# One layer of a hybrid encoder with 32 experts: the front part, up to the first projection, is redone

## What is computed

```python
cond = silu(c)
mod = cond @ w_ada + b_ada                     # D_MODEL = 1024, six parts
h = rmsnorm(x, norm1_g) * (1.0 + sc1) + sh1    # x: 256 x 1024
proj = h @ w_in + b_in
# the filters of the Hyena branch, which depend on no input x
hdn = sin(freq * (z @ w1 + b1))                # 256 x 64
hdn = sin(freq * (hdn @ w2 + b2))
hdn = sin(freq * (hdn @ w3 + b3))
filt = (hdn @ w4) * window                     # 256 x 2 orders x 2 directions x 512
# used as spectra: y = irfft(rfft(u) * rfft(kern))
```

## Time and profile before

| | us |
|---|---|
| median of three runs | 1292.68 |
| lowest and highest | 1291.25 to 1293.13 |
| the profiled execution: its time | 1291.79 |
| the profiled execution: its span | 1290.0 |

### The profile page before, as it was taken

How to read it: one execution, slowest core, us unless ns; L and a number is a source line. 1 busy time by engine, 2 the same in 40 slices (tenths; PEclk the granted TensorE clock), 3 DMA queues, 4 the chain that set the end, 5 groups by cost and what they waited for, 6 DMA issues and landing times.

```text
span 1290.0 us, 13991 instructions
## 1 busy us (share of the span) xinstructions
PE 1213.5 (94%) x5550; PEld 577.2 (45%) x5550; DVE 410.2 (32%) x774; ACT 174.0 (13%) x311; POOL 33.1 (3%) x50
## 2 busy tenths in 40 slices
PE   6999999999999999999999998999899999989897
PEld 1777478888544343333333332433333333334332
DVE  5178896884422221120222102111301211021203
ACT  3222004230221010010101001000101010010000
POOL 3300200001000000000000000000000000000000
PEclk9999999999999999999999999999999999999999
DMA  9943442779489999999999999999999999999996
GB/s 373 383 174 108 148 156 107 301 286 401 179 354 426 401 428 428 428 429 428 428 430 429 427 428 429 428 428 430 429 428 428 429 428 428 430 429 427 427 426 247
DMA packets 50707, 475.73 MB, mean 369 GB/s; under 512 B 3970, under 2 KB 4130, under 8 KB 24051
## 3 DMA queue, kind: packets, MB, share of 16 engines
q1 hardware_dynamic: 49426, 471.26, 87.8%
q0 software_dynamic: 1248, 4.03, 0.9%
HBM read 474.22 MB, written 1.05 MB: 368 GB/s over the span
## 4 chain that ended last, share of the span: by engine, by line
PE 66%; DMA 28%; DVE 2%; ACT 1%; issue 1%; SPq 0%; DVEq 0%
DMA ring_sb<-w_down 26%; PE bank L1149 20%; PE bank L1249 11%; PE bank L859 10%; PE bank L1104 5%; PE bank L1265 4%; PE bank L1020 3%; PE bank L868 3%; PE bank L1049 2%; DMA area_sb<-w_down 2%; PE bank L1118 1%; DVE area_sb L1867 1%; PE bank L784 1%; PE bank L798 1%; PE bank L1010 1%
## 5 line engine op out<-in xcount | busy, mean ns | idle before, releaser
L1149 PE MATMUL bank<-ring_sb,area_sb 128*64 128x512 f32 x1536 | 400.2, 598 | 16.4 <-DMA ring_sb<-w_gu 16.4
L1149 PEld LDWEIGHTS bank<-ring_sb,area_sb 128*64 128x64 f32 x1536 | 124.4, 137 | 226.1 <-issue 213.7
L1249 PE MATMUL bank<-ring_sb,area_sb 128*64 128x512 f32 x608 | 165.9, 598 | 18.7 <-DMA ring_sb<-w_down 16.8
L1149 PE MATMUL bank<-area_sb 128*64 128x512 f32 x512 | 171.2, 594 | 0.0
L859 PE MATMUL bank<-area_3h_sb,ring_sb 128*128 128x256 f32 x704 | 154.2, 379 | 0.0
L859 PEld LDWEIGHTS bank<-area_3h_sb,ring_sb 128*128 128x128 f32 x704 | 133.2, 190 | 20.1 <-issue 1.8
L2123 DVE TENSOR_SCALAR area_sb<-bank 128x512 f32<-128x512 f32 x32 | 22.1, 692 | 304.2 <-PE bank L1149 304.2
L2147 DVE TENSOR_TENSOR area_sb<-area_sb,bank 128x512 f32<-128x512 f32 x64 | 44.0, 688 | 211.9 <-PE bank L1265 211.9
L2154 DVE TENSOR_TENSOR area_sb<-bank,area_sb 128x512 f32<-128x512 f32 x32 | 22.1, 692 | 230.4 <-PE bank L1249 218.0
L1249 PEld LDWEIGHTS bank<-ring_sb,area_sb 128*64 128x64 f32 x608 | 51.2, 137 | 89.7 <-issue 89.7
L1509 ACT ACTIVATE area_sb<-bank 128x512 f32<-128x512 f32 (+1 forms) x80 | 44.0, 551 | 333.5 <-PE bank L1104 255.6
(11 more groups left out here) (278 smaller groups left out, 807.8 us busy)
## 6 DMA issues: line engine op xcount, KB each, us to landing
ring_sb<-w_gu SPq DMA_DIRECT2D x96, 2048.0 KB, 26.2
ring_sb<-w_down SPq DMA_DIRECT2D x38, 2048.0 KB, 25.8
area_sb<-w_gu SPq DMA_DIRECT2D x32, 2048.0 KB, 30.3
area_sb<-w_down SPq DMA_DIRECT2D x16, 2048.0 KB, 20.4
ring_sb<-w_in SPq DMA_DIRECT2D x14, 2048.0 KB, 10.1
ring_sb<-w_ada SPq DMA_DIRECT2D x12, 2048.0 KB, 10.3
area_3h_sb<-w_down SPq DMA_DIRECT2D x8, 2048.0 KB, 35.6
ring_sb<-w_branch SPq DMA_DIRECT2D x3, 2048.0 KB, 9.5
```

The lines of the kernel that those rows point to most:

```text
L1149: ins = pe.matmul(bank[n][r, :], xT[:, k, r], w[e][:, n * 512:(n + 1) * 512], start=False, stop=k == KT - 1, skip_group_check=True)
L1249: ins = pe.matmul(bank[4 + n][r, :], hidT[:, k, e * SLOTS:(e + 1) * SLOTS], w[e][:, kk, n * 512:(n + 1) * 512], start=False, stop=k == KT ...
```

## The change

- **Angles in turns.** The frequency is scaled by 1/(2 pi) once, so a layer's angle comes in turns; its nearest whole number is subtracted and ScalarE's sine takes the factor -2 x 3.1415925. Three VectorE steps a layer in place of seven.
- **Constant products.** TensorE multiplies `ones` by `ones` (128 columns) six, seven and nine times ahead of and between the network's products, into the bank of `ada3`, which a later product with its start flag clears.
- **Order.** TensorE: `mlp(2)`, `ada(0)`, filters, `ada(1)`, `spectrum(0)`, three parts of `spectrum(1)`, `ada(2)`, `xT`, `ada(3)`, `modcol`, the last part of `spectrum(1)`. VectorE windows all filters, adds the tap, and empties `spectrum(0)` itself, with the mean square after two of the four parts and the inverse root after the last. ScalarE does the second sine ahead of the tables and empties three parts of `spectrum(1)` behind the scaling of x.
- **Own buffer.** The parts of `spectrum(1)` go to `area_1`. GpSimd mixes the first spectrum as soon as it is emptied, half of the second after `xT3`, and the rest after its last part. The zeroing of the pads of `hy_in` waits for all eight mixes, and ScalarE waits for the pads later, ahead of `hyena_out`.

```diff
+    jobs += [(f"spectrum0{j}", "dve") for j in SPECTRUM_ORDER]
+    jobs += [(f"spectrum1{j}", "act") for j in SPECTRUM_ORDER[:3]]
...
-        split = view(area_4, 0, [4, W])
+        split = [view(area_4, 0, [4, W]), view(area_1, 0, [4, W])]
...
-            pool.wait_ge(modcol_ready, 1)
-            mix_kernel(0)
-            mix_kernel(1)
+            wait_emptied(pool, "spectrum00")
+            for n in (2, 3, 0, 1):
+                mix_kernel(0, n)
+            wait_emptied(pool, "spectrum11")
+            pool.wait_ge(products_ready, JOB["xT3"] + 1)
+            for n in (2, 3):
+                mix_kernel(1, n)
+            wait_emptied(pool, "spectrum10")
+            for n in (0, 1):
+                mix_kernel(1, n)
...
+            def fill(n):
+                for _ in range(n):
+                    pe.matmul(bank[BANK[JOB["ada3"]]][:, 0:P], ones[:, :], ones[:, :], start=True, stop=True)
+            fill(6)
             mlp(0)
+            fill(7)
             mlp(1)
+            fill(9)
+            mlp(2)
             ada(0)
-            mlp(2)
-            ada(1)
...
+            ada(1)
+            wait_emptied(pe, "filter011")
+            wait_emptied(pe, "filter111")
+            pe.wait_ge(tables_made, 2)
+            for n in SPECTRUM_ORDER:
+                if n == 1:
+                    pe.wait_ge(tap_biased, 1)
+                spectrum(0, n)
+            for n in SPECTRUM_ORDER[:3]:
+                spectrum(1, n)
             ada(2)
-            spectrum(0)
...
-            spectrum(1)
+            spectrum(1, SPECTRUM_ORDER[3])
...
-                act.activation(mlp_y[:, 3, :], mlp_y[:, 0, :], ACT.Sin).then_inc(sin_done, 1)
+                act.activation(mlp_y[:, 3, :], mlp_y[:, 0, :], ACT.Sin, scale=-2.0 * 3.1415925).then_inc(sin_done, 1)
...
-            spectrum_out(0)
+            for n in SPECTRUM_ORDER[:3]:
+                spectrum_out(n)
             copy_out("ada0", part[:, 0, :])
...
-                step(dve.tensor_scalar(turns, y, 1.0 / (2 * math.pi), ROUND, ALU.mult, ALU.add))
-                step.wait()
-                step(dve.tensor_scalar(turns, turns, -ROUND, None, ALU.add))
-                for part_of_pi in (PI_A, PI_B, PI_C):
-                    step.wait()
-                    step(dve.scalar_tensor_tensor(y, turns, -part_of_pi, y, ALU.mult, ALU.add))
-                step.wait()
-                dve.tensor_scalar(y, y, 3.1415925, -3.1415925, ALU.min, ALU.max).then_inc(sin_asked, 1)
+                step(dve.tensor_scalar(turns, y, ROUND, None, ALU.add))
+                step.wait()
+                dve.scalar_tensor_tensor(y, turns, -ROUND, y, ALU.add, ALU.subtract).then_inc(sin_asked, 1)
...
             windowed(0, 0)
             windowed(0, 1)
-            dve.wait_ge(x_squared, TT)
-            step(dve.tensor_scalar(x_ms, x_ss, 1.0 / D, EPS, ALU.mult, ALU.add))
-            step.wait()
-            dve.sem_inc(sqrt_asked, 1)
             windowed(1, 0)
-            inverse_root(1, x_ms, x_rt, x_r, x_t)
-            dve.sem_inc(r_ready, 1)
             windowed(1, 1)
...
             dve.tensor_tensor(taps, taps, hy_bias, ALU.add).then_inc(tap_biased, 1)
+            spectrum_out(SPECTRUM_ORDER[0])
+            spectrum_out(SPECTRUM_ORDER[1])
+            dve.wait_ge(x_squared, TT)
+            step(dve.tensor_scalar(x_ms, x_ss, 1.0 / D, EPS, ALU.mult, ALU.add))
+            step.wait()
+            dve.sem_inc(sqrt_asked, 1)
+            spectrum_out(SPECTRUM_ORDER[2])
+            spectrum_out(SPECTRUM_ORDER[3])
+            inverse_root(1, x_ms, x_rt, x_r, x_t)
+            dve.sem_inc(r_ready, 1)
...
+            dve.wait_ge(kernel_mixed, 8)
+            dve.memset(hy_in[:, :, 0:1], 0.0)
+            dve.memset(hy_in[:, :, SEQ + 1:SEQ + 2], 0.0).then_inc(pads_zeroed, 1)
             wait_emptied(dve, "cg1")
```

## The result

| | before | changed |
|---|---|---|
| median of the runs taken together (18 each) | 1291.14 us | 1297.53 us |
| lowest and highest | 1289.39 to 1293.88 | 1292.87 to 1301.44 |
| the profiled execution: time, span | 1291.79, 1290.0 | 1300.25, 1298.5 |
| inverse root of x, first to last step | 0.95 | 5.1 |
| `ada3` starts | 33.87 | 40.31 |

The changed kernel is slower: ratio 1.0044, 95% interval 1.0035 to 1.0054. The forecast was 1293.1 with a range of 1288.9 to 1296.0. It was built on the median of three runs of the kernel before, 1292.68; the eighteen give 1291.14. The profiled execution of the changed kernel, 1300.25, lies 2.7 us above its median.

The account below looks back on a forecast made before the run. Bound: start of `cg0`, then fixed TensorE work, then the expert-weight stream. Shorter angles, held root and low clock put `cg0` 0.45 later: 1291.79 + 0.45 + 0.89 = 1293.1 us, chance 0.36, own range 1291.0 to 1295.0, overall 1288.9 to 1296.0.

Parts of the forecast that it names:

- The floor: Earliest start of `cg0`, when chunk 4 with its weights lands at 37.3: at most 4.45 us gained.
- `cg0` itself: Start of `cg0`: 41.3 by the sum, 42.2 with the clock term, 0.45 us later than before.
- I take the first: Constant products' own cost, between -0.5 us (higher clock by about 9) and +2 (all low): -0.5 taken.
- 15.1: Start of the filters after the shortened angles, instead of 21.48: 6.4 us earlier.
- the fourth rival: Fills don't lift the clock, network late by 1 to 2 us: 1294 to 1295, chance 0.06.
- The network's steps: Starts of the second and third network products, forecast at 8.9 and 12.45.
- The clock behind the gap: Idle TensorE ahead of the transposes lowers its clock: `ada3` up to 1.7 us longer, 0.9 taken.
- three lost: Inverse root beside GpSimd's mix: first multiply passes, three steps held up to 1.24 us each, root ends at 30.0.
- filters and spectra: From the filters' start at 15.1 through window products, tap and spectrum 0 to its last eviction at 25.9.
- The third rival: All four root steps held and clock low, `cg0` 2.6 to 4.2 us later: 1295.3 to 1296.9, chance 0.16.
- Three steps a layer: VectorE's angle takes three steps a layer instead of seven, 1.85 us a layer instead of 3.41.
- The pads: Zeroing of the pads waits for all eight mixes, covered with 8 us to spare: no cost.

Follow-up runs that it names:

- e5: Kernel before with four GpSimd additions put beside the inverse root of x: median 1295.8 us, ratio 1.0046 to the kernel before.
- e6: Kernel before with two GpSimd additions put beside the inverse root of x: median 1293.7 us, ratio 1.0021 to the kernel before.
- e8: Kernel before with constant products alone, six ahead of the first network product and twelve ahead of the second: median 1292.2 us, ratio 1.0017.
- e4: Changed kernel without its constant products: median 1297.2 us, ratio 1.0044 to the kernel before.
- e3: Changed kernel with 19 more constant products on TensorE between `ada2` and `xT0`: median 1295.1 us, ratio 1.0021 to the kernel before.
- e1: Changed kernel with GpSimd's first mix also waiting for the inverse root of x: median 1290.9 us, ratio 0.9996 to the kernel before.
- e2: Changed kernel with the root's four steps as eight one-column, one-tensor-input instructions, mix still beside them: median 1291.5 us, ratio 0.9989 to the kernel before.
- e11: Kernel of e10 with four constant products instead of nine ahead of the third network product: median 1288.4 us, ratio 0.9979 to the kernel before.
- e9: Changed kernel with four constant products instead of nine ahead of the third network product: median 1295.0 us, ratio 1.0036 to the kernel before.
- e10: Changed kernel, mean square ahead of the tap, root ahead of spectrum 0's evictions, two spectrum 1 parts (not three) ahead of `ada2`: median 1288.2 us, ratio 0.9981.

## Why the prediction was wrong

**What bounds the kernel: right.** A shift of `cg0` by 6.18 is one of 6.23 at the expert loop and of 6.4 by the medians. The experiments, with `cg0` between 38.6 and 47.9, follow it to 1 or 2 us, apart from e5, e6 and e8, whose profiled executions were the lowest or highest of their kernels. The floor (chunk 4 at 37.3) wasn't reached, and no wait of TensorE for a chunk came up between `cg0` and the loop.

**`cg0` itself: forecast 42.2, measured 47.93.** The 5.7 us are three terms of the sum, in order of size:

1. *Constant products, "I take the first" (-0.5 us): wrong sign.* I had expected the higher level by about 9. The network products took 1.12, 1.12 and 0.76, the level rose only by 15, the seven fills made the second product 0.9 late (9.83 against 8.9), and the nine took 4.14 us against a wait of 2. The filters started at 17.66, not 15.1: 2.6 us, the fourth rival, to which I gave 0.06 and only 1 to 2 us. I had priced their half-clock length, and yet took the end at which it doesn't occur. The network's steps were right: without fills (e4) the second and third product started at 8.69 and 12.52, forecast 8.9 and 12.45. But the 15.1 also needed `ada0` at full clock, which e4 didn't have: against no fills at all, the fills cost only 0.6 us at the filters.
2. *The clock behind the gap, "0.9": measured 2.85* (1.74 in `xT`, 1.11 in `ada3`; e3 gives 2.9 at `cg0`). I counted only `ada3`, as if ScalarE still paced the transposes. At half clock they take 3.65 us, and ScalarE's three evictions end at 37.56, so TensorE is what paced them. The miss is 1.9 us.
3. *The root, "three lost": four.* The first multiply came 0.03 us behind GpSimd, not ahead. Root 5.1 instead of the 4.1 of the forecast: 1.0 us. The mechanism, the place and one step per GpSimd instruction were as forecast, and e1, e2, e5 and e6 show it. The forecast rested on rows with GpSimd's `TENSOR_TENSOR`, and the mix is one.

2.6 + 1.9 + 1.0 = 5.5; the rest is in the filters and spectra (below). These terms are read from one execution, one of the slower ones.

The range failed because I treated late fills as a rival that excludes the held steps and the low clock, with a time of its own, while all three add: held steps make the gap, the gap takes the clock, and the fills are late whatever follows. The third rival (1295.3 to 1296.9) with the fourth's 1 to 2 us on top gives 1296.3 to 1298.9, which holds the measured 1297.5, but with luck: the fills cost 2.6, and all my times stood on a median of the kernel before that was 1.5 too high (1292.68 against 1291.14). The same 1.5 made the miss in the time smaller, 4.4 us.

**The rest.** Three steps a layer: right. The pads: VectorE zeroed them at 51.8, 4 us behind `cg0`, covered. Filters and spectra behind 17.66 ran by the sum: last eviction at 28.78, that is 11.1 behind the filters' start, forecast 10.8.

## What to carry to other kernels

Before moving small steps of VectorE, look at what GpSimd does beside them: beside GpSimd instructions with two SBUF inputs, a chain of n dependent steps with two SBUF inputs loses up to n of them, and ordering them one after the other costs a single wait. Where TensorE is made to wait longer, price the clock for all that follows, the transposes too. And when unknown costs can occur together, add their bad ends for the range; they are no rivals.

## What the runs showed of the hardware

- A VectorE step on two columns took 1.2 us instead of 0.16 beside a GpSimd addition of 512 columns, and the same arithmetic on one column with a per-partition scalar took 0.17. The order of start, 0.02 to 0.04 us apart, decided whether the first was held (held in four traces, passed in two).
- Beside a GpSimd `TENSOR_SCALAR` of 384 columns, a VectorE instruction with two SBUF inputs wasn't held: 0.43 us for 256 columns, as when alone.
- Constant products raised TensorE's level after very different times. The trace has no clock record there; by the durations it rose some 2.8 us after the first of them in e8, 3.5 in e11, 8.3 in e9, and 12.3 to 12.9 in the changed kernel, e1, e2, e3 and e10. All of them begin with the same six products at 2.64 or 2.65. What makes the difference isn't settled by these runs.
- With the level up early (e8, e11) TensorE waited 2.1 and 1.8 us ahead of a narrow network product, and behind it the granted clock fell to 0.50, 0.5 and 0.2 us into `ada0`, which then took 3.21 and 3.54 us.
